# Projecting the second mixer's q, k, gates and branches with stationary weights, inside a longer attention loop

## The reference

```
proj = x @ w_in                                   # 1024 -> 2304 + 2048
q_na, k_na, v_na, q_sw, k_sw, v_sw, gate_logits = split(proj)
y_na = neighbourhood_attention(q_na, k_na, v_na, rpb)      # 8 heads of 64, a bias table per head
y_sw = sliding_window_attention(rotary(q_sw), rotary(k_sw), v_sw, sink)   # 8 heads, 2 for k and v
g_na, g_sw = split(sigmoid(gate_logits + b_gate))          # 1024 each
out = (g_na * (y_na @ w_branch_na) + g_sw * (y_sw @ w_branch_sw)) @ w_out
x = layer_norm(ALPHA * x + out)
```

## Time and profile before

| | |
|---|---|
| median of three runs | 2499.74 us |
| the profiled execution | 2504.72 us |
| its span | 2502.9 us |
| granted TensorE clock over it | 0.961 of full speed |
| TensorE busy (matmuls) | 2322.3 us, 93% |
| VectorE busy | 1740.1 us, 70% |
| ScalarE busy | 1448.2 us, 58% |
| GpSimd busy | 217.4 us, 9% |
| DMA | 572.91 MB, mean 229 GB/s |

### The profile page before, as it was taken

One profiled execution on the slowest core, in us unless ns is written; L12 is line 12 of the kernel. 1 busy time (PEld: TensorE's weight loads), 2 busy tenths in 40 slices (PEclk: granted clock), 3 DMA queues, 4 the chain that ended last, 5 costly groups with the idle time before them and its releaser, 6 DMA issues. The chain is left out here.

```text
span 2502.9 us, 30180 instructions
## 1 busy us (share of the span) xinstructions
PE 2322.3 (93%) x11198; PEld 1941.3 (78%) x11198; DVE 1740.1 (70%) x2390; ACT 1448.2 (58%) x2061; POOL 217.4 (9%) x133
## 2 busy tenths in 40 slices
PE   6878998888999899799899879999999999999997
PEld 5777887777788678688678768888888888888885
DVE  5854555783555535555543658989898989898988
ACT  4444444443444445344444447878787878787876
POOL 1321000231000141000014000000000000000000
PEclk9989999988999999899999979999999999999999
DMA  6314554512555543455453339999999999999996
GB/s 249 126 34 143 183 188 157 186 60 76 170 189 188 183 134 111 143 182 189 158 199 117 118 110 337 371 340 370 341 369 339 373 343 364 342 371 345 365 349 240
DMA packets 157751, 572.91 MB, mean 229 GB/s; under 512 B 18560, under 2 KB 18880, under 8 KB 156960
## 3 DMA queue, kind: packets, MB, share of 16 engines
q1 hardware_dynamic: 154000, 555.58, 63.4%
q0 software_dynamic: 3600, 15.35, 1.8%
HBM read 569.80 MB, written 1.05 MB: 228 GB/s over the span
## 5 line engine op out<-in xcount | busy, mean ns | idle before, releaser
L398 DVE TENSOR_TENSOR w_lo<-raw,w_hi 128x1024 fp32r<-128x1024 f32 x995 | 1200.8, 1224 | 357.6 <-ACT w_hi L392 330.6
L392 ACT CAST w_hi<-raw 128x1024 fp32r<-128x1024 f32 x1055 | 1102.4, 1051 | 409.6 <-PE bank L458 392.9
L456 PE MATMUL bank<-w_hi,x_hi 128*128 128x512 f32 (+3 forms) x2872 | 1137.4, 396 | 28.0 <-DVE arena L1383 6.5
L458 PE MATMUL bank<-w_hi,x_lo 128*128 128x512 f32 (+3 forms) x2872 | 1115.0, 388 | 0.0
L457 PE MATMUL bank<-w_lo,x_hi 128*128 128x512 f32 (+3 forms) x2872 | 1113.3, 388 | 0.0
L456 PEld LDWEIGHTS bank<-w_hi,x_hi 128*128 128x128 f32 x2872 | 547.0, 190 | 134.8 <-DVE arena L1383 7.3
L458 PEld LDWEIGHTS bank<-w_hi,x_lo 128*128 128x128 f32 x2872 | 545.0, 190 | 110.5
L457 PEld LDWEIGHTS bank<-w_lo,x_hi 128*128 128x128 f32 x2872 | 546.9, 190 | 100.7
L398 POOL TENSOR_TENSOR w_lo<-raw,w_hi 128x1024 fp32r<-128x1024 f32 x60 | 143.4, 2390 | 296.1 <-ACT w_hi L392 296.0
L538 POOL TENSOR_SCALAR small<-small 128x2 f32<-128x2 f32 x9 | 7.1, 794 | 1852.1 <-ACT arena L529 1573.0
L1356 ACT CAST x_hi<-bank 128x256 fp32r<-128x256 f32 x112 | 41.8, 374 | 83.1 <-PE bank L1759 43.8
(11 more groups left out here) (202 smaller groups left out, 1428.7 us busy)
## 6 DMA issues: line engine op xcount, KB each, us to landing
raw<-in_stream SPq DMA_DIRECT2D x1055, 512.0 KB, 5.7
tab<-in_lngb POOLq DMA_DIRECT2D x5, 1024.0 KB, 5.1
arena<-in_rpb POOLq DMA_DIRECT2D x16, 256.0 KB, 5.7
arena<-in_bgate POOLq DMA_DIRECT2D x4, 512.0 KB, 4.7
tab<-in_rowv POOLq DMA_DIRECT2D x2, 640.0 KB, 8.8
X<-in_x SPq DMA_DIRECT2D x1, 1024.0 KB, 5.0
out_y<-X SPq DMA_DIRECT2D x2, 512.0 KB, 2.9
tab<-in_ropec POOLq DMA_DIRECT2D x2, 448.0 KB, 5.0
```

Source lines behind the costliest of these rows:

```text
L392: nc.scalar.copy(w_hi[:, s % SPLIT, :], raw[:, slot, :]).then_inc(hi_done, 1)
L398: e.tensor_tensor(w_lo[:, s % SPLIT, :], raw[:, s % RAW, :], w_hi[:, s % SPLIT, :].bitcast(F32), ALU.subtract).then_inc(done, 1)
L456: pe.matmul(out, xh, wh, start=first, stop=False)
L458: return pe.matmul(out, xl, wh, start=False, stop=last)
```

## The change

Only the second mixer's program and what serves it is changed. Line numbers below 470 shift by 16.

- q_na, k_na, the gates and both branches are projected with the weights stationary and x (or O) moving, 256 tokens at once (`rows_halves`, `branch_half`, `both3`): a half is 24 matmuls of 256 columns where it was 12 of 512. The outputs have features on rows. q_na and k_na are split straight from their banks into `qk_t` and `qk_l` (`projected`), the gates take their bias as a column in ScalarE's evacuation (`gates_out`; `bias_columns` makes those columns with one transpose from a small DMA in place of two broadcasts of it).
- Before the loop stand q_na, k_na (4 halves each) and v_na (4 halves of 512 columns). The projection of q_sw, k_sw, v_sw, the rotary and its 10 transposes move into the loop.
- What each of the loop's 18 steps takes is set by `fill`: steps 0 to 3 q_sw, 4 and 5 k_sw with v_sw, 6 to 13 two gate halves each, 14 and 15 a half of the neighbourhood branch, 16 none, 17 two of that branch. O is transposed pair by pair of heads in the loop (`pair_unit` at steps 9, 11, 13, 16, 17), the sigmoid stands at steps 15 and 17 in two pieces of 128 x 2048.
- After the loop: the gates times the neighbourhood branch on VectorE (`na_gates`, 4 instructions), four halves of the sliding-window branch (`sw_half`), four times `gated`: VectorE multiplies, adds, ScalarE writes `x_hi`, VectorE `x_lo`; and the 8 output halves, whose operand has features on rows already, so that the transposes of YG are gone. An output half waits for its `gated` (`yg_lo`).
- `attention`: TensorE's wait for the banks' evacuations goes from the loop's head to map 0's PV; the scores wait for `proj_lo` where they waited for `qk_lo`.

The order of the weight stream and its number of halves stay as they are.

The cut diff (`+` and `-` lines; "..." where lines are left out):

```diff
+            if E.kind == "pe" and "made" not in maps[0]:
                 e.wait_ge(qk_lo, E.qk.at())
-                wait(e, acc_act, E.acc.at())
-                wait(e, acc_dve, E.acc.at())
+                wait(e, acc_act, values)
+                wait(e, acc_dve, values)
...
+                        if m == 0:
+                            wait(e, acc_act, values)
+                            wait(e, acc_dve, values)
...
+            turned_at, maps_before = [], E.map.at()
...
+            def both3(out, wh, wl, xh, xl, first, last):
+                e.matmul(out, wh, xh, start=first, stop=False, skip_group_check=True)
+                e.matmul(out, wh, xl, start=False, stop=False, skip_group_check=True)
+                return e.matmul(out, wl, xh, start=False, stop=last, skip_group_check=True)
...
+            def rows_halves(b0, fresh=False):
                 for hx in range(KD // 2):
...
+                            if fresh:
+                                need(E, k)
+                            for j in range(512 // P):
+                                w = slice(i2 * 512 + j * P, i2 * 512 + (j + 1) * P)
+                                i = both3(region(b0, j), wh[:, w], wl[:, w], x_hi[:, k, :], x_lo[:, k, :],
+                                          j % 2 == 0 and k == 0, j % 2 == 1 and k == KD - 1)
                         return i
                     E.half_step(use)
                     yield
...
+            def projected(b0, blk, scale, fresh=False):
+                for _ in rows_halves(b0, fresh):
+                    pass
+                if E.kind in ("act", "dve"):
+                    if E.kind == "act":
+                        e.wait_ge(w_used, E.st.done(-1))
+                    for j in range(2):
+                        hi, lo = pair_of(blk + 2 * j, 2)
+                        src = bank[b0 + j][:, :].rearrange("p (b n) -> p b n", n=S)
+                        if E.kind == "act":
+                            nc.scalar.mul(hi, src, scale).then_inc(proj_hi, 1)
+                        else:
+                            e.wait_ge(proj_hi, n_proj + blk // 2 + j + 1)
+                            e.scalar_tensor_tensor(lo, src, scale, hi.bitcast(F32), ALU.mult,
+                                                   ALU.subtract).then_inc(proj_lo, 1)
...
+            def gates_out(b0, c):
+                if E.kind == "act":
+                    if c == 0:
+                        e.wait_ge(bc_done, l + 1)
+                    e.wait_ge(w_used, E.st.done(-1))
+                    for j in range(512 // P):
+                        b = c * (512 // P) + j
+                        nc.scalar.activation(GT[:, b, :], region(b0, j), ACT.Identity,
+                                             bias=bcol[:, b:b + 1]).then_inc(gate_raw, 1)
...
+            def sigmoid(half):
+                if E.kind == "act":
+                    e.wait_ge(gate_raw, n_gate + N_GATE)
+                    g = GT[:, half * KD:(half + 1) * KD, :]
+                    nc.scalar.activation(g, g, ACT.Sigmoid).then_inc(gate_done, 1)
...
+            def pair_unit(bk, p):
+                if E.kind == "pe":
+                    e.wait_ge(o_done, maps_before + 2 * p + 2)
+                unit(E, bk, pair_of(p, 1), [lambda tb: O[:, tb, p * P:(p + 1) * P]], lag=2)
...
+            def branch_half(banks, k, first, last, full=None):
+                def use(wh, wl):
...
+                            w = slice(b * P, (b + 1) * P)
+                            i = both3(bank[bk][:, j * S:(j + 1) * S], wh[:, w], wl[:, w], OT_hi[:, k, :],
+                                      OT_lo[:, k, :], first and j == 0, last and j == 1)
+                        if full is not None and bk != banks[-1]:
+                            i.then_inc(full, 1)
+                    return i
+                E.half_step(use)
...
+            def na_half(k):
+                if E.kind == "pe" and k == 0:
+                    e.wait_ge(qk_lo, E.qk.at())
+                    e.wait_ge(gate_raw, n_gate + N_GATE)
+                branch_half((6, 7, 4, 5), k, k == 0, k == N_NA - 1)
...
+            def sw_half(k):
+                if E.kind == "pe":
+                    e.wait_ge(qk_lo, E.qk.at())
+                branch_half((0, 1, 2, 3), N_NA + k, k == 0, k == N_NA - 1, sw_full if k == N_NA - 1 else None)
...
+            def na_gates(at):
...
+                if E.kind == "dve":
+                    e.wait_ge(gate_done, 2 * l + 1)
+                    e.wait_ge(w_used, at)
+                    for j in range(4):
+                        g = GT[:, 2 * j:2 * j + 2, :]
+                        i = e.tensor_tensor(g, bank[4 + j][:, :].rearrange("p (b n) -> p b n", n=S), g, ALU.mult)
...
+                    e.engine_nop().then_inc(na_gated, 1)
...
+            def gated(j):
...
+                g, z = GT[:, KD + 2 * j:KD + 2 * j + 2, :], GT[:, 2 * j:2 * j + 2, :]
+                b = slice(2 * j, 2 * j + 2)
+                n = (KD // 2) * l + j + 1
+                if E.kind == "dve":
+                    e.wait_ge(gate_done, 2 * l + 2)
+                    if j < 3:
+                        e.wait_ge(sw_full, 3 * l + j + 1)
+                    else:
+                        e.wait_ge(w_used, E.st.done(-1))
+                    E.link(e.tensor_tensor(g, bank[j][:, :].rearrange("p (b n) -> p b n", n=S), g, ALU.mult))
+                    e.tensor_tensor(z, z, g, ALU.add).then_inc(yg_src, 1)
+                    e.wait_ge(yg_hi, n)
+                    e.tensor_tensor(x_lo[:, b, :], z, x_hi[:, b, :].bitcast(F32), ALU.subtract).then_inc(yg_lo, 1)
+                if E.kind == "act":
+                    e.wait_ge(yg_src, n)
+                    nc.scalar.copy(x_hi[:, b, :], z).then_inc(yg_hi, 1)
...
+            def out_half(k):
+                if E.kind == "pe":
+                    e.wait_ge(yg_lo, (KD // 2) * l + k // 2 + 1)
+                    if k == 0:
+                        e.wait_ge(na_gated, l + 1)
...
+                            i = mm3(e, bank[4 + 2 * tb + c][:, :], x_hi[:, k, t], x_lo[:, k, t], wh[:, w], wl[:, w],
...
+            projected(4, 0, HD ** -0.5, fresh=True)
+            bias_columns()
+            projected(6, N_NA, 1.0)
...
+                e.wait_ge(proj_lo, n_proj + 2)
+            for _ in token_halves(4, 2 * W_NA, W_NA):
+                pass
...
+            sw_q, sw_kv = token_halves(6, C_QS, SH * HD), token_halves(4, C_KS, 2 * SKV * HD)
+            gates = [rows_halves(6 - c % 2 * 2) for c in range(4)]
...
+            def fill(step):
+                if step < 4:
+                    if step == 0 and E.kind == "pe":
+                        e.wait_ge(proj_lo, n_proj + N_NA)
+                    next(sw_q)
+                if step in (4, 5):
+                    if step == 4 and E.kind == "pe":
+                        wait(e, acc_act, E.acc.at())
+                        wait(e, acc_dve, E.acc.at())
+                    next(sw_kv)
+                if step == 5:
+                    rotary()
+                if 6 <= step < 14:
+                    c = (step - 6) // 2
+                    if step % 2 == 0 and E.kind == "pe":
+                        e.wait_ge(qk_lo, E.qk.at())
+                        wait(e, gate_raw, n_gate + 4 * c - 4)
+                    next(gates[c])
+                    if step == 6:
+                        turned_unit(4, 0, 2)
+                        turned_unit(5, 2, 2)
+                    if step == 7:
+                        turned_unit(4, sg, 1)
+                        turned_at.append(E.qk.at())
+                    if step in (9, 11, 13) and E.kind == "pe":
+                        e.wait_ge(gate_raw, n_gate + 4 * c)
+                    if step == 9:
+                        pair_unit(6, 0)
+                        pair_unit(7, 1)
+                    if step == 11:
+                        pair_unit(4, 2)
+                        pair_unit(5, 3)
+                    if step == 13:
+                        pair_unit(6, 4)
+                    next(gates[c])
+                    if step % 2 == 1:
+                        gates_out(6 - c % 2 * 2, c)
+                if step in (14, 15):
+                    na_half(step - 14)
+                if step == 15:
+                    sigmoid(0)
+                if step == 16:
+                    pair_unit(0, 5)
+                    pair_unit(1, 6)
+                if step == 17:
+                    na_half(2)
+                    sigmoid(1)
+                    pair_unit(0, 7)
+                    na_half(3)
+                pool_bias(E, l, step)
...
+            attention(E, maps, fill)
+            na_gates(E.st.done(-1))
+            for k in range(N_NA):
+                sw_half(k)
+            for j in range(KD // 2):
+                gated(j)
+            for k in range(KD):
+                out_half(k)
             if E.kind == "dve":
-                e.engine_nop().then_inc(tp_src, 1)
-            tp_stage(E, O[:, :, 0:D], KD, 0)
...
```

(12 more changed lines are left out.)

208 lines of the change are left out of this document (107 added, 101 removed).

## The result

The changed kernel takes **2472.77 us** (median of four runs, 2472.58 to 2472.86), the one before 2499.38 in the runs beside it (2497.37 to 2501.48). The ratio is 0.9894, 95% interval 0.9882 to 0.9905: 26.6 us less, where 26.1 less and 2473.6 us were forecast. The total is right. Two things behind it are not, and they go in opposite ways: the changed loop was charged too long, and the profile of the kernel before that the sum starts from held more low clock than most of its executions do.

A forecast was written before the change was run, and what follows sets the result against it. TensorE was taken to bound projections, loop and branches. Per mixer 35.0 + 117.3 + 38.0 = 190.3 us replaced 203.4, 26.1 us less in both, so the median 2499.74 would become 2473.6 us; range 2465 to 2487.

The forecast's parts named there:

- the join: Stage between projections and loop, 9.48 us with TensorE waiting for rotary and low parts: removed, with the low clock behind it.
- Before the loop: Projection stage: 12 halves of q_na, k_na and v_na remain, plus low clock at the start; 35.0 us.
- The loop: Attention loop: grows from 86.18 to 117.3 us with added halves and transposes, TensorE kept busy.
- the 3.2 us of transposes: In the loop: 10 transposes of q_sw and k_sw and 16 of O at 0.123 us each.
- 0.8 of breaks: In the loop: seven places where TensorE changes kind of work, 0.11 us each.
- the 39.1 us of the rest: In the loop: the maps' own work with its breaks, taken to stay unchanged at 39.1 us.
- The tail: After the loop: sliding-window branch 11.5, wait 2.5, output 21.8, wait 1.8, odd 0.4; 38.0 us.
- wait 1.8: At the fourth output half: TensorE waits 1.8 us for its weight split, queued on VectorE behind all four gated.
- the 2.5 us gap: Before the output: TensorE waits 2.5 us for x; no low clock charged, and a clock falling there would show error.
- The loop did stay TensorE's: Rival in the loop: changed-order steps wait; in half, 11.3 us, 2485 (chance 0.13); in all, 22.7 us, 2496 (0.04).
- The stationary loads: Slower rival, 256-column matmuls: each costs its load's 0.19 us, not 0.12; 41 us more a mixer, 2581; chance 0.04.
- The gating is short: Rival before the output: gating keeps up to its 5.92 us wait, 3.4 us a mixer more, 2480; chance 0.07.

The follow-up runs named there:

- the run with 256 columns: Kernel before, each gate half as 24 matmuls of 256 columns instead of 12 of 512, x still stationary; 2504.80 us, ratio 1.0018.
- The second profile: Kernel before, unchanged, run and profiled once more; median 2499.61 us, ratio 1.0002, profiled execution 2497.2 us.
- both together: Changed kernel with VectorE's gated 0 ahead of the sliding-window branch's last half and weight splits between the other gated; 2468.82 us, ratio 0.9882 to the kernel before.
- the chain cut: Changed kernel with first gated early and cut in two, weight splits placed before each is needed; 2467.57 us, repeated 2465.63 us.
- the splits between: Changed kernel with VectorE's and ScalarE's weight splits for output halves 3 to 5 placed between the four gated; 2474.50 us, ratio 0.9905 to the kernel before.
- the wait at the loop's head: Changed kernel with TensorE's wait for v_na's evacuation put back to the loop's head; 2477.85 us, ratio 0.9908 to the kernel before.
- the branch behind the loop: Changed kernel with the neighbourhood branch's four halves moved behind the loop; 2486.66 us, ratio 0.9943 to the kernel before.
- the transposes behind it: Changed kernel with O's transposes of pairs 4 to 7 moved behind the loop, before the sliding-window branch; 2476.17 us, ratio 0.9903 to the kernel before.
- the early `gated`: Changed kernel with VectorE's part of gated 0 placed before its split for output half 2; 2474.18 us, ratio 0.9908 to the kernel before.

## Why the prediction was right, and where it was not

**What bounds, and the join.** Right. The rows of the join stage are gone, the scores' first matmul starts 0.32 us after v_na's last one does, the clock is 1.00. Before the loop: 35.0 forecast, 35.28 measured.

**The loop.** 117.3 forecast, 115.4 measured, the first mis-sized term. The 3.2 us of transposes were counted from 16 transposes in 1.97 us; the seven groups in the loop take 0.79, 0.14, 0.35, 0.35, 0.13, 0.79 (with a wait of 0.18) and 0.14 us to the next row's start, 2.5 without the wait: 0.7 less. The 26 halves, each from its first row to the next work's first, take 77.5 us. Charged were 78.4: 74.2 at steady pitch, 0.8 of breaks, and 3.4 that lay in the 39.1 us of the rest, 16 times the 0.21 to 0.22 us of a half of 512 columns between other work. That is 0.9 less, 0.7 of it because a half of 256 columns at the head of a step costs 0.10 and not 0.16 more than one of 512, as the run with 256 columns shows, in twelve steps. The maps' own work took 0.4 less than before, and the wait of 0.18 had not been charged. Together 1.8 or 1.9, what was seen. That ScalarE, VectorE and GpSimd would keep up was right, and the wait for O fell from 0.63 to 0.18 us.

**The tail.** 38.0 forecast, 11.73 + 2.28 + 23.68 = 37.7 measured, but for another reason. The step that has TensorE want the fourth half at 13.6 us and wait 1.8 took a full clock behind the 2.5 us gap, for which the prediction charged nothing, with the earlier trace rows as the nearest row. The gap does drop the clock in both mixers of both profiles, and in 11 of the 12 mixers of six traces in which it was 2.3 us. The 1.8 is also more than the prediction's own terms give: 15.0 to 15.3 less 13.6 is 1.4 to 1.7. Where the clock stayed, 1.23 us were measured. The runs showed the two costs to be alternatives behind this gap, 1.44 us of clock or 1.2 of lateness, so the sum was right although its clock was wrong. That is luck: the prediction did not see that one cost would stand in for the other. A clock that falls after the 2.5 us gap had been named as a sign of being wrong; it fell, and the total did not move.

**The base of the sum.** The prediction put the 5 us between the profiled execution and the median down to the execution, and subtracted 26.1 from both. The second profile shows that a part of those 5 us lay in what the change removes: its mixers are 1.66 and 4.00 us shorter than those read. Against the first profile the mixers gained 15.0 and 15.5 us, against the second 13.3 and 11.5. The low clock of 3.0 us at the loop's head, charged as always there, came in four of six loops of the kernel before and its 256-column form. In the first layer of the second profile the difference is mostly the output's clock, in the second the loop head's. This overcount of the gain and the 3.8 us overcount of the changed loops' length cancelled, which is luck as well.

**The rivals.** The loop did stay TensorE's. The stationary loads don't show: 0.120 us a matmul, in the changed kernel too (900.88 to 903.51 in its trace is 22 distances of 0.1195, and the loads' rows are 0.19 us long there). The Trainium skill ("TensorE: Matmul & The Clock Gate", The mechanism) says in one place that a load overlaps running matmuls "only when row_grp differs", in another that one into the background weight buffer does too. The first by itself is not what these traces show. The Trainium skill's 262 and 518 cycles (same page, Back-to-back issue gap) are for a single isolated matmul; by them the two forms would differ by 0.03 us a half. 0.16 was measured in a run of such halves and 0.10 in the loop. The gating is short, and shorter still once it stands ahead of the split.

## What to carry to other kernels

When work is taken off the way between two matmul phases, count the chain that is left (here 2.8 us of multiply, add, cast, subtract) and ask what stands in front of it on its engine: a split of weights that nobody wanted yet cost 1.1 to 1.5 us of gap and, with it, the clock. Two costs behind one another can hide each other; removing one alone showed nothing in two of these runs, and only both together paid, 4.9 us in the two mixers and 7.1 with the chain cut. And a gain that includes a low clock should be taken from more than one profile, since after gaps of the same length it came in some layers and not in others.

## What the runs showed of the hardware

- The same gap, from the same work, is followed by the lower clock level in some executions and not in others. After 2.3 us of waiting before the output it fell in 11 of 12 mixers (the changed kernel twice, the splits between, the wait at the loop's head, the branch behind the loop, and one layer of the transposes behind it) and stayed in the other layer of the last. At 2.32 and 2.35 us before the fourth half it stayed and fell. Behind the waits of 0.80 to 1.15 us (the early `gated`, and the loop's head) it stayed in all six mixers. In three traces of the kernel before and its 256-column form it fell in four of six loops. Where it falls it costs 1.4 to 1.6 us in the output and 3.06 at the loop's head.
- A half between other work takes longer than its steady pitch, and less so with 256 columns (0.16 us over 2.88) than with 512 (0.22 over 2.72).
- Transposes between two halves cost 0.11 us each, whatever their number: a step's two halves last 5.91 to 5.93 us without any, 6.13 with two, 6.36 with four and 6.79 with eight between them.
